# A hybrid decoder layer: the decays of a recurrence head move into the head's own step, and four norms share one run of logarithms

## The reference

```python
z = rms_norm(x, norm_mix) @ w_in            # 7 blocks of 1024 columns: q_a, k_a, v_a, q_r, f_r, i_r, g_r
# group A, 8 heads: norm of q and k, rotary, causal differential attention (two score maps), norm of the output
p = softmax(s, axis=-1); w = p[:, :, 0] - lam * p[:, :, 1]
# group B, 8 heads: a gated linear recurrence
log_f = log(lbf + (1.0 - lbf) * sigmoid(zf))
k_r = (1.0 - lbf) * sigmoid(-zf)
b = cumsum(log_f); q_dec = q * exp(b)
o = causal(q_dec @ (k * exp(-b))) @ v + q_dec @ S
S_new = exp(b_last) * S + (k * exp(b_last - b)) @ v
o_rnn = rms_norm(o_rnn, rnn_gain) * silu(g_r)
x = x + concat(o_att, o_rnn) @ w_out
x = x + conv_ffn(rms_norm(x))                # silu(conv3(h W_gate)) * (h W_up), then W_down
x = x + sigmoid(rms_norm(x) @ w_ple_gate) * (p @ w_ple_proj)
```

## Time and profile before

| | us |
|---|---|
| median of 3 runs | 2974.2 (2973.12 to 2978.13) |
| the profiled execution, its own time | 2973.09 |
| span of that execution's instructions | 2971.3 |
| one step of the loop over heads (span 392.66 to 511.81) | 119.15 |
| PE busy over the span | 98% |
| DVE, ACT, POOL busy | 50%, 36%, 3% |

### The profile page before, as it was taken

How to read it: one execution, slowest core, us unless ns; L and a number is a source line. 1 busy time by engine, 2 the same in 40 slices (tenths; PEclk the granted TensorE clock), 3 DMA queues, 4 the chain that set the end, 5 groups by cost and what they waited for, 6 DMA issues and landing times.

```text
span 2971.3 us, 53260 instructions
## 1 busy us (share of the span) xinstructions
PE 2909.2 (98%) x19995; PEld 2670.5 (90%) x19995; DVE 1499.3 (50%) x2411; ACT 1068.2 (36%) x1481; POOL 96.4 (3%) x75
## 2 busy tenths in 40 slices
PE   6999999999999999999999999999999999999998
PEld 6888888888888899899999999999999999998998
DVE  5455453554444645544554444544445545455544
ACT  4355454454543523422233222332223322234332
POOL 2011010110100100000000000000000000000000
PEclk9999999999999999999999999999999999999999
DMA  5333333333333533233233332333322323323332
GB/s 196 93 105 98 96 96 97 106 99 88 94 103 101 172 113 86 80 92 92 85 92 94 92 92 84 93 96 90 92 87 88 102 85 92 92 84 93 99 106 85
DMA packets 546618, 291.78 MB, mean 98 GB/s; under 512 B 15208, under 2 KB 537570, under 8 KB 546378
## 3 DMA queue, kind: packets, MB, share of 16 engines
q1 hardware_dynamic: 515482, 268.88, 31.0%
q10 hardware_dynamic: 31040, 21.46, 2.3%
HBM read 268.83 MB, written 21.63 MB: 98 GB/s over the span
## 4 chain that ended last, share of the span: by engine, by line
PE 92%; DVE 4%; ACT 2%; issue 2%; SPq 0%; DMA 0%; DVEq 0%; ACTq 0%
PE product L883 26%; PE product L887 14%; PE product L885 14%; PE product L884 14%; PE product L886 13%; PE scratch L698 2%; PE scratch L706 2%; PE scratch L747 1%; DVE w_lo L1429 1%; PE scratch L792 1%; PE scratch L769 1%; PE scratch L752 1%; ACT L1057 1%; PE scratch L697 1%; DVE r_km L1632 1%
## 5 line engine op out<-in xcount | busy, mean ns | idle before, releaser
L883 PE MATMUL product<-act,w_hi 128*128 128x512 f32 x2816 | 1151.6, 409 | 37.1 <-DVE act L1656 15.0
L1429 DVE TENSOR_TENSOR w_lo<-w_raw,w_hi 128x1024 fp32r<-128x1024 f32 (+1 forms) x496 | 607.5, 1226 | 580.2 <-ACT w_hi L1046 580.1
L1046 ACT ACTIVATE w_hi<-w_raw 128x1024 fp32r<-128x1024 f32 (+1 forms) x496 | 514.2, 1037 | 978.7 <-PE product L887 957.0
L887 PE MATMUL product<-act,w_lo 128*128 128x264 f32 x2816 | 808.0, 287 | 0.0
L885 PE MATMUL product<-act,w_hi 128*128 128x264 f32 x2816 | 803.3, 285 | 0.0
L884 PE MATMUL product<-act,w_hi 128*128 128x264 f32 x2816 | 802.2, 285 | 0.0
L886 PE MATMUL product<-act,w_lo 128*128 128x256 f32 x2816 | 794.6, 282 | 0.0
L885 PEld LDWEIGHTS product<-act,w_hi 128*128 128x128 f32 x2816 | 533.1, 189 | 128.7
L883 PEld LDWEIGHTS product<-act,w_hi 128*128 128x128 f32 x2816 | 535.8, 190 | 55.3 <-issue 22.2
L884 PEld LDWEIGHTS product<-act,w_hi 128*128 128x128 f32 x2816 | 535.6, 190 | 3.4 <-issue 1.9
L887 PEld LDWEIGHTS product<-act,w_lo 128*128 128x128 f32 x2816 | 534.6, 190 | 0.0
(11 more groups left out here) (249 smaller groups left out, 2526.6 us busy)
## 6 DMA issues: line engine op xcount, KB each, us to landing
w_raw<-in_w_in SPq DMA_DIRECT2D x112, 512.0 KB, 3.8
w_raw<-in_w_gate SPq DMA_DIRECT2D x88, 512.0 KB, 3.8
w_raw<-in_w_up SPq DMA_DIRECT2D x88, 512.0 KB, 3.8
w_raw<-in_w_down SPq DMA_DIRECT2D x64, 384.0 KB, 3.4
w_raw<-in_w_down SPq DMA_DIRECT2D x64, 320.0 KB, 3.2
w_raw<-in_w_out SPq DMA_DIRECT2D x32, 512.0 KB, 3.9
w_raw<-in_w_ple_gate SPq DMA_DIRECT2D x32, 384.0 KB, 3.4
k_pages<-in_cache_k SPq DMA_DIRECT2D x128, 64.0 KB, 2.8
```

Of the source, the lines that this page charges most:

```text
L883: pe.matmul(both, hi, x[:, k, :, 0:TA], start=begin, stop=False)
L887: mm = pe.matmul(far, lo, x[:, k, 1, TA:T], start=False, stop=end)
L1046: act.activation(w_hi[:, slot, 0:n, :], w_raw[:, slot, 0:n, :], ACT.Copy).then_inc(w_hi_ready, 1)
L1429: dve.tensor_tensor(flat(w_lo[:, slot, 0:n, :]), flat(w_raw[:, slot, 0:n, :]), flat(w_hi[:, slot, 0:n, :]).bitcast(F32), ALU.subtract).the ...
```

## The change

In words: the two tables get new slots, and the last step a table of its own (`RECURRENCE_ALONE`). The recurrence tasks of head r fill slots 0 to 8 of the step of head r + 1. The decays of head h are made in the step of head h itself, in slots 17, 18 and 20 (the f block has been read at slot 16), on POOL as well, whose last two products now also wait for the r block. `ssq_q` and `ssq_k` stand together in slot 10, `ssq_r` and `ssq_a` in slot 11; ACT takes their logarithms one after another and then the four exponentials, and DVE normalizes in slot 12. `att_out` moves from slot 25 to 27, where `ssq_a` was; `ssq_a` is made one step later. The product with the gate (`gate_r`) stands at slot 18. Plans with an odd number of tasks get one small padding task at their end (head 0 and the last step).

```diff
 ATTENTION = {
-    6: ["ssq_q"], 8: ["rot_q"], 10: ["ssq_k"],
-    12: ["rot_k"], 13: ["pages0"], 14: ["pages1", "v_nat"], 15: ["k_nat", "score0"],
-    16: ["s_score"], 17: ["score1"], 18: ["w0"], 19: ["s_prob", "score2", "w1"],
-    21: ["score3"], 22: ["w2"], 24: ["w3", "s_out"], 25: ["s_turn", "att_out"], 27: ["ssq_a"],
+    10: ["ssq_q", "ssq_k"], 12: ["pages0"], 13: ["pages1", "rot_q"], 14: ["rot_k"], 15: ["v_nat", "k_nat"],
+    16: ["score0", "s_score"], 17: ["score1"], 18: ["w0"], 19: ["s_prob", "score2", "w1"],
+    21: ["score3"], 22: ["w2"], 24: ["w3", "s_out"], 25: ["s_turn"], 27: ["att_out"],
 }
 RECURRENCE = {
-    3: ["i_nat"], 7: ["kh_nat"], 9: ["upd"], 11: ["intra"], 14: ["rnn"], 16: ["s_upd"], 18: ["s_rnn"], 20: ["ssq_r"],
+    0: ["i_nat"], 1: ["kh_nat"], 2: ["upd"], 3: ["intra"], 5: ["rnn"], 7: ["s_upd"], 8: ["s_rnn"], 11: ["ssq_r", "ssq_a"],
+}
+RECURRENCE_ALONE = {
+    0: ["ssq_a", "i_nat", "kh_nat", "upd", "intra"], 3: ["rnn"], 5: ["s_upd"], 7: ["s_rnn"], 10: ["ssq_r"],
 }
...
# ACT, in step
-                if r is not None and s == 0:
-
-                    act.wait_ge(*evacuated("f", r))
+                if h is not None and s == 17:
+
+                    act.wait_ge(*evacuated("f", h))
                     func(r_k[:, :], z_f[:, :], ACT.Sigmoid, scale=-1.0)
                     func(z_f[:, :], z_f[:, :], ACT.Sigmoid).then_inc(flag("sig_f"), 1)
+                if r is not None and s == (17 if h is not None else 12):
+
+                    act.wait_ge(flag("r_normed"), r + 1)
                     act.wait_ge(*evacuated("g", r))
-                    func(r_g[:, :], z_g[:, :], ACT.Sigmoid).then_inc(flag("sig_g"), 1)
-                    act.wait_ge(flag("f_done"), r + 1)
+                    func(mix_r[:, :], z_g[:, :], ACT.Sigmoid).then_inc(flag("sig_g"), 1)
+                if h is not None and s == 17:
+                    act.wait_ge(flag("f_done"), h + 1)
                     func(r_kh[:, :], z_f[:, 0:SEQ], ACT.Ln).then_inc(flag("log_f"), 1)
-                if r is not None and s == 2:
-                    act.wait_ge(flag("b_left"), r + 1)
+                if h is not None and s == 18:
+                    act.wait_ge(flag("b_left"), h + 1)
                     func(r_kh[:, :], r_kh[:, :], ACT.Exp).then_inc(flag("exp_left"), 1)
-                    act.wait_ge(flag("b_mid"), r + 1)
+                    act.wait_ge(flag("b_mid"), h + 1)
                     func(r_qm[:, :], r_qm[:, :], ACT.Exp).then_inc(flag("exp_mid"), 1)
-                if r is not None and s == 4:
-                    act.wait_ge(flag("mid_b"), r * SUBS + SUBS)
+                if h is not None and s == 20:
+                    act.wait_ge(flag("mid_b"), h * SUBS + SUBS)
...
+                if h is not None and s == 12:
+
+                    beside = ["ssq_r", "ssq_a"] if r is not None else []
+                    for name in beside:
+                        log_sum(name, it)
+                    for name in ["ssq_q", "ssq_k"] + beside:
+                        inv_root(name, it)
...
# DVE, in step: the same decays from r and slots 0 and 2 to h and slots 17 and 18, and
+                if h is not None and s == 12:
+                    small("norm_q", it, h, r)
+                    small("norm_k", it, h, r)
+                if r is not None and s == (12 if h is not None else 10):
+                    small("norm_r", it, h, r)
+                if r is not None and h is not None and s == 12:
+                    small("norm_a", it, h, r)
+                if r is not None and s == (18 if h is not None else 12):
+                    small("gate_r", it, h, r)
```

More of the change, by code:

```diff
@@ L107, in tasks_of @@
     plan = []
+    of_recurrence = RECURRENCE if attention else RECURRENCE_ALONE
     for s in range(HALVES):
-        plan.append((RECURRENCE.get(s, []) if recurrence else []) + (ATTENTION.get(s, []) if attention else []))
+        plan.append((of_recurrence.get(s, []) if recurrence else []) + (ATTENTION.get(s, []) if attention else []))
     return plan
 def late_parts(plan, s):
-    late = ["late_" + name for name in plan[s - 1] if name.startswith("score")] if s > 0 else []
-    return (["late_ssq_r"] if s > 1 and "ssq_r" in plan[s - 2] else []) + late
+    return ["late_" + name for name in plan[s - 1] if name.startswith("score")] if s > 0 else []
 class Scratch:
@@ L552, in step @@
                         x_back(HEADS + j - 4)
-                if attention and s == (10 if r is None else 6):
+                if s == (10 if r is None else 4):
                     if r is None:
@@ L780, in small @@
             elif name == "ssq_a":
-                wide(name, it, [("sq_a", n)], K("ones"), sq)
+                wide(name, it, [("sq_a", m)], K("ones"), mix_a)
             elif name == "kh_nat":
@@ L1057, in func, with log_sum, inv_root @@
             return act.activation(out, in_, f, **kw)
+        SUMS = {"ssq_q": (rr, DK, "rr_q"), "ssq_k": (sq, DK, "rr_k"), "ssq_a": (mix_a, P, "rr_a"), "ssq_r": (mix_r, P, "rr_r")}
+        def log_sum(name, it):
+            dst, count, _ = SUMS[name]
+            b = take(name, it)
+            func(two(dst[:, :]), m_wide(b), ACT.Ln, scale=1.0 / count, bias=K("eps")).then_inc(free[b], 1)
+        def inv_root(name, it):
+            dst, _, sig = SUMS[name]
+            act.wait_ge(*read(name, it))
+            func(dst[:, :], dst[:, :], ACT.Exp, scale=-0.5).then_inc(flag(sig), 1)
         def small(name, it, h, r):
@@ L1061, in small @@
             m = None if r is None else r + 1
[L1062 to L1086, removed]
+            if name in ("ssq_q", "ssq_k"):
+                log_sum(name, it)
+            elif name in ("ssq_a", "ssq_r"):
+                if h is None:
+                    log_sum(name, it)
+                    inv_root(name, it)
             elif name in ("pages0", "pages1"):
@@ L1135, in small @@
                 act.wait_ge(free[sb_], sv)
-                func(sq[:, :], oT[:, :], ACT.Square).then_inc(flag("sq_a"), 1)
+                if r is not None:
+                    act.wait_ge(flag("mix_a_out"), r * 16 + 16)
+                func(mix_a[:, :], oT[:, :], ACT.Square).then_inc(flag("sq_a"), 1)
             elif name == "i_nat":
@@ L1219, in step @@
                     act.wait_ge(*evacuated("k", h))
-                    func(sq[:, :], z_k[:, :], ACT.Square).then_inc(flag("sq_k"), 1)
-                if h is not None and s == 10:
+                    func(sq_k[:, :], z_k[:, :], ACT.Square).then_inc(flag("sq_k"), 1)
+                if h is not None and s == 12:
+                    beside = ["ssq_r", "ssq_a"] if r is not None else []
+                    for name in beside:
+                        log_sum(name, it)
+                    for name in ["ssq_q", "ssq_k"] + beside:
+                        inv_root(name, it)
+                if h is not None and s == 14:
                     act.wait_ge(flag("q_rot_done"), h + 1)
@@ L1572, in small @@
                 t.then_inc(free[b], 1)
[L1573 removed]
+            elif name == "norm_r":
                 dve.wait_ge(flag("rr_r"), m)
[L1575 to L1576 removed]
+                dve.scalar_tensor_tensor(r_o[:, :], r_o[:, :], vec(ROWS_A["rnn"]), mix_r[:, :], ALU.mult, ALU.mult).then_inc(flag("r_normed"), 1)
+            elif name == "gate_r":
+                dve.wait_ge(flag("sig_g"), m)
+                dve.tensor_tensor(z_g[:, :], z_g[:, :], mix_r[:, :], ALU.mult).then_inc(flag("r_gate"), 1)
                 dve.wait_ge(flag("r_gate"), m)
@@ L1902, in visit @@
                 if h0 == 0:
-                    return
-                if h1 == HEADS:
+                    step(plan, 0, 0, None)
+                elif h1 == HEADS:
                     with pool.Fori(h0, h1) as h:
                         step(plan, h - 1, h, h - 1)
-                else:
-                    step(plan, 0, None, HEADS - 1)
         phases(visit)
```

91 lines of the change are left out of this document (43 added, 48 removed).

## The result

| | before | changed |
|---|---|---|
| median of four runs, us | 2973.75 (2973.12 to 2978.13) | 3052.64 (3051.55 to 3053.62) |
| span of the profiled execution, us | 2971.3 | 3050.6 |
| a step of the loop (h = 3), us | 119.3 | 129.5 |

The changed kernel is slower by 79 us, a ratio of 1.0262 with a 95% interval of 1.0244 to 1.0280.

The account below looks back on a forecast made before the run. PE, busy 98% of the span, was taken as the bound. Seven steps 84.7, head 0 10.1, `w_lo` wait -11.8, padding +1, last step +2: together +86.0 us, so 3060, range 3022 to 3088.

Parts of the forecast that it names:

- item 7: In the ordered ACT and DVE work of slots 17 to 20: `r_qm`, 1.7 us, expected to run beside POOL's `r_kh`.

Follow-up runs that it names:

- e1: Changed kernel with ACT's copy of `w0` put before the exponentials of `r_kh` and `r_qm` in slot 18: 3057.8 us.
- e5: Changed kernel with ACT's copy of `w0` before the exponentials of `r_kh` and `r_qm`, and `gate_r` moved from slot 18 to 21 in the loop: 3036.6 us.
- e4: Kernel before, with the four `r_km` differences moved from slot 2 to 4 and their exponentials from slot 4 to 6: 2961.5 us.
- e8: e4 with TensorE's loop over heads written out: 2954.7 us.
- e10: e9 with TensorE's loop over heads written out: 2956.0 us.
- e3: Changed kernel with decays in slots 24, 26, 27 instead of 17, 18, 20, `gate_r` in 24, write of `mix_r` in 26: 2978.4 us.
- e9: e3 with ACT's write of `mix_r` in slot 25 instead of 26, TensorE's branch kept: 2981.0 us.
- e12: e10 with `intra`, `rnn`, `s_upd`, `s_rnn` in slots 5, 7, 8, 9 instead of 3, 5, 7, 8: 2960.6 us.

## What to carry to other kernels

When work is moved into a stretch, add up what stands in order on each queue between two points that TensorE must pass, and compare that with TensorE's own work between them; an engine that is idle half of the step on average can be full just there. Relieving the longest wait is worth nothing while another queue ends at the same place (e1), so try the parts together as well (e5). At a loop's back edge, a wait that the trace puts down to another engine may be the loop's own: writing out one engine's loop tests it in one edit.

## What was not expected of the hardware

- **DVE and POOL side by side.** `r_qm` (DVE) and `r_kh` (POOL) overlap in both kernels. In the loop before, POOL began 0.07 us earlier in all seven steps: `r_qm` took 1.76 to 1.78 us and POOL's product 1.29. In the changed kernel DVE began 0.07 to 0.16 us earlier in all eight: `r_qm` took 0.68 to 0.69 and POOL's product 1.65 to 1.74. Which of the two was slowed went with which began first. The four `r_km` behind `r_qm` take 1.69 in e4, where POOL is idle beside them, and 2.76 in the changed kernel, where POOL's `r_kh` runs on 1.14 us beyond the end of `r_qm`. The Trainium skill (SBUF — State Buffer, SBUF: two separate sides) has the rule that the two engines take a port pair in turns and the one that starts first keeps it for its whole instruction; the trace agrees, and item 7 should have been priced by the order of the starts. Here is POOL's product, first before (the earlier trace rows has the `r_qm` beside it), then in the changed kernel:

```profile
405.80 1.29 POOL L1866 TENSOR_TENSOR r_kh<-r_k,r_kh 128x512 f32<-128x512 f32 x1 [107.41 <-ACT r_kh L1057]
```

```profile
510.59 1.74 POOL L1877 TENSOR_TENSOR r_kh<-r_k,r_kh 128x512 f32<-128x512 f32 x1 [103.62 <-ACT r_kh L1056]
```

- **The back edge.** Between kernels the length of the wait varied with the task before it: with `ssq_a`, four wide matmuls, in front of the back edge PE stood 0.7 to 1.3 us (before and e4), with the twenty short ones of `att_out` 1.5 to 2.0, and with the loop written out 0.34 in e8 and none in e10. Why the task before matters is left open.
- **The clock after small tasks.** A product behind `intra` took 4.1 to 5.4 us instead of 2.96, at no wait, in one to six of seven loop steps, in the kernel before too. Single runs of some versions differ by 10 us and more (e3, e9, e12), and the mean granted clock goes with it: in e12 it was 0.982 in the run of 2979.6 us and 0.989 to 0.990 in those near 2960. Whether it is this product in those runs is not shown.
